# Decay matrices of a state-space scan: running sums spread by DMA and masked on GpSimd, in place of products on TensorE

## What is computed

```python
def _decay_matrix(a_cs):
    q = a_cs.shape[-1]
    mask = jnp.tril(jnp.ones((q, q), dtype=bool))
    diff = a_cs[..., :, None] - a_cs[..., None, :]
    return jnp.exp(jnp.where(mask, diff, -jnp.inf))
...
    decay_in = _decay_matrix(jnp.moveaxis(a_cs, 2, -1))
    cb = jnp.einsum('bclgn,bcsgn->bcgls', cc, bc)
    y_diag = jnp.einsum('bcgls,bcghls,bcsghp->bclghp', cb, decay_in, xdt)
    y_off = jnp.einsum('bclgn,bcghpn,bclgh->bclghp', cc, h_prev, jnp.exp(a_cs))
    return (y_diag + y_off).reshape(bsz, l, N_HEADS, HEAD_DIM)
```

## Time and profile before

| | us |
|---|---|
| median of 3 runs | 2501.23 |
| the runs | 2499.74, 2505.65, 2501.23 |
| the profiled execution: span of its instructions | 2505.4 |
| the profiled execution: its own time, the only one of the three that can hold the span | 2505.65 |
| PE busy, weight loads beside it | 2452.1, 1669.5 |
| DVE, ACT, POOL busy | 1099.7, 904.6, 167.6 |

### The profile page before, as it was taken

The page is one execution under the profiler, slowest core; times in us unless marked ns, Lnnn a source line. Parts: engine busy times, 40 slices in busy tenths (PEclk is TensorE's granted clock), DMA queues, the critical chain, the costliest instruction groups (busy, mean ns, idle before and its releaser), DMA issues.

```text
span 2505.4 us, 31969 instructions
## 1 busy us (share of the span) xinstructions
PE 2452.1 (98%) x13068; PEld 1669.5 (67%) x13068; DVE 1099.7 (44%) x1700; ACT 904.6 (36%) x1446; POOL 167.6 (7%) x162
## 2 busy tenths in 40 slices
PE   8999999999999999999999999999999999999998
PEld 7888778888888688898977888444444444444343
DVE  6446575455455755567866645221111111111111
ACT  5436454444444554466654643211101111101111
POOL 0000200000002000051600000000000000000000
PEclk9999999999999999999999999999999999999999
DMA  7546765555556665443422347999999999999997
GB/s 271 185 168 214 273 217 187 184 194 189 183 202 234 246 231 179 145 152 118 169 101 85 127 150 267 392 431 430 431 431 430 432 431 431 430 430 431 431 431 327
DMA packets 72805, 688.34 MB, mean 275 GB/s; under 512 B 8338, under 2 KB 8482, under 8 KB 12288
## 3 DMA queue, kind: packets, MB, share of 16 engines
q1 hardware_dynamic: 69696, 675.98, 69.1%
q0 software_dynamic: 3008, 10.95, 1.3%
HBM read 683.76 MB, written 1.05 MB: 273 GB/s over the span
## 4 chain that ended last, share of the span: by engine, by line
PE 82%; DMA 9%; DVE 4%; ACT 3%; issue 2%; POOL 0%; SPq 0%; ACTq 0%; DVEq 0%
PE bank L446 39%; PE bank L3018 21%; DMA work<-in_stream 4%; DMA ring<-in_stream 4%; PE bank L2965 4%; PE bank L1921 4%; PE bank L3007 2%; PE bank L484 2%; ACT split_r L401 1%; DVE work L1979 1%; PE bank L2321 1%; PE bank L764 1%; DVE ring_r L412 1%; PE bank L1100 1%; PE bank L1302 1%
## 5 line engine op out<-in xcount | busy, mean ns | idle before, releaser
L412 DVE TENSOR_TENSOR ring_r<-ring,split_r 128x2048 fp32r<-128x2048 f32 (+1 forms) x211 | 474.7, 2274 | 345.2 <-ACT split_r L401 345.1
L446 PE MATMUL bank<-split_r,xT_r 128*128 128x512 f32 (+1 forms) x1760 | 546.2, 388 | 1.8 <-ACT work L1426 1.7
L401 ACT CAST split_r<-ring 128x2048 fp32r<-128x2048 f32 (+1 forms) x228 | 429.3, 1904 | 160.3 <-PE bank L446 125.0
L446 PEld LDWEIGHTS bank<-split_r,xT_r 128*128 128x128 f32 x1760 | 328.7, 188 | 70.1 <-issue 2.3
L446 PE MATMUL bank<-ring_r,xT_r 128*128 128x512 f32 (+1 forms) x880 | 339.5, 386 | 0.0
L446 PE MATMUL bank<-split_r,work_r 128*128 128x512 f32 x960 | 301.0, 391 | 0.5 <-DVE ring_r L412 0.4
L3018 PE MATMUL bank<-ring,work 128*64 128x512 f32 x1152 | 261.1, 602 | 4.3 <-DMA ring<-in_stream 2.7
L446 PEld LDWEIGHTS bank<-split_r,work_r 128*128 128x128 f32 x960 | 180.3, 188 | 38.0 <-DVE ring_r L412 0.9
L446 PE MATMUL bank<-ring_r,work_r 128*128 128x512 f32 x480 | 186.9, 389 | 0.0
L446 PEld LDWEIGHTS bank<-ring_r,xT_r 128*128 128x128 f32 x880 | 165.4, 188 | 31.9
L3018 PEld LDWEIGHTS bank<-ring,work 128*64 128x64 f32 x1152 | 79.6, 138 | 154.8 <-issue 147.2
(11 more groups left out here) (409 smaller groups left out, 3063.7 us busy)
## 6 DMA issues: line engine op xcount, KB each, us to landing
ring<-in_stream SPq DMA_DIRECT2D x256, 1024.0 KB, 5.0
ring<-in_stream SPq DMA_DIRECT2D x72, 2048.0 KB, 27.0
split<-in_stream SPq DMA_DIRECT2D x48, 2048.0 KB, 27.8
xT<-in_stream SPq DMA_DIRECT2D x24, 2048.0 KB, 27.4
work<-in_stream SPq DMA_DIRECT2D x24, 2048.0 KB, 28.2
x<-in_stream SPq DMA_DIRECT2D x24, 1024.0 KB, 25.7
work<-in_stream SPq DMA_DIRECT2D x24, 1024.0 KB, 28.3
row<-in_rows POOLq DMA_DIRECT2D x6, 512.0 KB, 4.3
```

The source lines that it names most:

```text
L401: act.copy(hi, self.part(half, self.ring)).then_inc(*up("half_hi", half.h))
L412: dve.tensor_tensor(self.part(half, self.ring_lo), self.part(half, self.ring), hi.bitcast(F32), ALU.subtract).then_inc(*up("half_lo", half.h))
L446: mm = self.nc.tensor.matmul(out, a[x][a_at], w[y][w_at], start=start and n == 0, stop=stop and n == 2)
```

## The change

The running sums are now spread to all partitions by DMA. PE makes them once for each chunk and direction, with 64 rows. ACT copies them to SBUF as they are, POOL writes them to a DRAM tensor `acs_rows`, and for each unit POOL issues a DMA (`pool_seg`) that reads 8 rows of 128 and writes them to all 128 partitions: 4 KB a partition, 512 KB in all. There are three such buffers. POOL then adds the mask, in two halves of 128x512 (`pool_masked`), ACT takes the exponentials in place (`act_decays`), DVE multiplies in place (`dve_decays`), and the diagonal products read the same buffer. Units 0 and 1 use the space of the fourth split buffer, unit 2 the convolution's.

The mask and sum products leave PE, and DVE's `acs_lo` and `acs_wide` go. In unit u PE makes B times C of unit u + 1 after the state product, and ACT and DVE make the decays of unit u + 1: ACT after its split, DVE ahead of `y_sum`. `off` and the diagonal products change between two banks each, so their waits go back two units instead of one. POOL's order in the scan is: masks of u, then the DMA for u + 2, which waits for the diagonal products of u - 1. A few waits and constants move with it (the second gates wait for `cbT` 15 and `y_sum` 14 instead of the exponentials; a zero-weight tile is now written with the identity).

```diff
...
+        self.acs_rows = nc.dram_tensor("acs_rows", (2, MT * NH2, P), F32, kind="Internal").ap()
...
-                self.n_hi, self.hi_user[N_HI - 1] = N_HI, (-1, ("seg", 15, 1))
+                self.n_hi, self.hi_user[N_HI - 1] = N_HI, (-1, ("diag", 15))
...
-        self.acs_T = wr(12288, 2, P)
-        self.acs_wide = [view(self.split[N_HI - 1], d * 1024, 8, P) for d in range(2)]
+        assert at + 3 * KD + 3 * P <= self.base
+        self.acs_T = w(12288, 2, P)
+        self.seg = [view(self.split_f, (N_HI - 1) * HALF + i * 1024, 8, P) for i in range(2)] + [w(11264, 8, P)]
...
-        for src, dst in ((self.ident, self.ident_r), (self.con["neg_f"], self.neg_r[0]), (self.con["neg_b"], self.neg_r[1]),
-                         (self.con["group_of"], self.group_r)):
-            i = act.copy(dst, src)
-        i.then_inc(*up("masks", 0))
+        for i in range(MT):
+            act.copy(self.w_of_none[:, i * P:(i + 1) * P], self.ident)
+        act.copy(self.ident_r, self.ident).then_inc(*up("masks", 0))
...
         for m in range(MT):
-            for part in range(2):
-                rows = slice(64 * m + 32 * part, 64 * m + 32 * part + 32)
-                for d, tri in ((0, self.con["tri_f"]), (1, self.con["tri_b"])):
-                    mm = pe.matmul(self.bank[5][rows, d * P:(d + 1) * P], dA[:, m, d, :], tri, start=True, stop=True)
+            rows = slice(NH2 * m, NH2 * (m + 1))
+            for d, tri in ((0, self.con["tri_f"]), (1, self.con["tri_b"])):
+                mm = pe.matmul(self.bank[5][rows, d * P:(d + 1) * P], dA[:, m, d, :], tri, start=True, stop=True)
         mm.then_inc(*up("acs_turned", 0))
...
     def act_acs_hi(self):
         act, at, up = self.nc.scalar, self.s.at, self.s.up
         act.wait_ge(*at("acs_turned", 0))
-        act.copy(self.acs_T, self.bank[5][:, 0:2 * P].rearrange("p (d n) -> p d n", d=2)).then_inc(*up("acs_hi", 0))
-
-    def dve_acs_lo(self):
...
-    def dve_acs_wide(self, d):
...
+        rows = slice(0, MT * NH2)
+        act.copy(self.acs_T[rows], self.bank[5][rows, 0:2 * P].rearrange("p (d n) -> p d n", d=2)).then_inc(*up("acs_hi", 0))
+
+    def pool_acs_out(self):
+
+        pool, at, up = self.nc.gpsimd, self.s.at, self.s.up
+        pool.wait_ge(*at("acs_hi", 0))
+        pool.dma_start(self.acs_rows.rearrange("d r n -> r d n"), self.acs_T[0:MT * NH2]).then_inc(*up("dma_acs", 0))
+
+    def pool_seg(self, u):
+
+        pool, at, up = self.nc.gpsimd, self.s.at, self.s.up
+        d, m, g = self.units[u]
+        if u == 0:
+            pool.wait_ge(*at("dma_acs", 0))
+            pool.wait_ge(*at(*self.wide_after))
+        elif u == 2:
+            pool.wait_ge(*at("conv_turned", 55))
+        elif u > 2:
+            pool.wait_ge(*at("diag", u - 3))
+        rows = self.acs_rows[d, NH2 * m + 8 * g:NH2 * m + 8 * g + 8, :].rearrange("h n -> (h n)")
+        pool.dma_start(flat(self.seg[u % 3]), rows.partition_broadcast(P)).then_inc(*up(f"dma_seg{u % 3}", u))
+
+    def pool_masked(self, u):
+
+        pool, at, up = self.nc.gpsimd, self.s.at, self.s.up
+        d, m, g = self.units[u]
+        pool.wait_ge(*at(f"dma_seg{u % 3}", u))
+        for half in range(2):
+            e = self.seg[u % 3][:, 4 * half:4 * half + 4]
+            pool.tensor_tensor(e, e, spread(self.con["neg_b" if d else "neg_f"], 1, 4), ALU.add).then_inc(*up("masked", u, half))
 
...
-            elif n == 36:
-                self.dve_acs_lo()
-            elif n in (43, 45):
-                self.dve_acs_wide((n - 43) // 2)
...
         for h in self.by_pool:
+            if h == self.first_piece - 28 + 20:
+                self.pool_acs_out()
+            elif h == self.first_piece - 28 + 23:
+                self.pool_seg(0)
+                self.pool_seg(1)
             self.pool_split(h)
...
         pool.wait_ge(*at("h0", 0, 3))
         pool.wait_ge(*at("h0", 1, 3))
         for g in range(NG2):
+            if g == 2:
+                self.pool_masked(0)
             pool.wait_ge(*at("turn_out", 43 + 4 * g))
...
+    def pe_cb(self, u):
+        pe, at, up = self.nc.tensor, self.s.at, self.s.up
+        d, m, g = self.units[u]
+        tok = slice(m * P, (m + 1) * P)
+        if u:
+            pe.wait_ge(*at("cbT", u - 1))
+        pe.matmul(self.bank[2][:, 0:P], self.BT[d][:, g, tok], self.CT[d][:, g, tok], start=True, stop=True).then_inc(*up("cb", u))
+
     def pe_unit(self, u):
         pe, at, up, bank = self.nc.tensor, self.s.at, self.s.up, self.bank
         d, m, g = self.units[u]
         tok = slice(m * P, (m + 1) * P)
...
+        off, y = bank[4 + u % 2], bank[(3, 6)[u % 2]]
+        if u == 0:
+            for w in (("turn_out", 54), ("turn_out", 55), ("dt", "dX", 1), ("masks", 0), ("h0", 0, 3), ("h0", 1, 3)):
                 pe.wait_ge(*at(*w))
-        pe.matmul(bank[4][:, 0:P], self.BT[d][:, g, tok], self.CT[d][:, g, tok], start=True, stop=True).then_inc(
-            *up("cb", u))
-        for half in range(2):
-            if u:
-                pe.wait_ge(*at("dec_exp", u - 1, half))
-            pe.matmul(bank[2 + half][:, :].rearrange("p (h l) -> p h l", h=4), self.ident_r, spread(self.neg_r[d], 1, 4),
-                      start=True, stop=False)
-            mg = m * NG2 + g
-            pe.matmul(bank[2 + half][:, :].rearrange("p (h l) -> p h l", h=4), self.group_r[:, mg:mg + 1].broadcast_to([P, P]),
-                      self.acs_wide[d][:, 4 * half:4 * half + 4], start=False, stop=True).then_inc(*up("seg", u, half))
-        if u:
-            pe.wait_ge(*at("yo", u - 1))
+            self.pe_cb(0)
+        if u >= 2:
+            pe.wait_ge(*at("yo", u - 2))
         if u % 4 >= 2:
             pe.wait_ge(*at("h1", u - 2))
-        pe.matmul(bank[5][:, :], self.CT[d][:, g, tok], self.h_st[d][:, g * 512:(g + 1) * 512], start=True,
+        pe.matmul(off[:, :], self.CT[d][:, g, tok], self.h_st[d][:, g * 512:(g + 1) * 512], start=True,
                   stop=True).then_inc(*up("off", u))
         if u % 4 < 2:
             pe.wait_ge(*at("xw", u))
             if u >= 4 or u % 4:
                 pe.wait_ge(*at("h1", u - 1 if u % 4 else u - 3))
             pe.matmul(bank[7][:, :], self.B[:, d, g * P:(g + 1) * P], self.xw, start=True, stop=True).then_inc(*up("state", u))
+        if u + 1 < 16:
+            self.pe_cb(u + 1)
         for p in self.pieces[u] if u else ():
             self.pe_piece(p)
-        if u:
-            pe.wait_ge(*at("y_sum", u - 1))
+        if u >= 2:
+            pe.wait_ge(*at("y_sum", u - 2))
         for half in range(2):
             pe.wait_ge(*at("decay", u, half))
             for hh in range(4):
                 h = 4 * half + hh
-                mm = pe.matmul(bank[6][:, h * HD2:(h + 1) * HD2], self.dec[half][:, hh, :],
+                mm = pe.matmul(y[:, h * HD2:(h + 1) * HD2], self.seg[u % 3][:, h, :],
                                self.X[:, m, g * 512 + h * HD2:g * 512 + (h + 1) * HD2], start=True, stop=True)
         mm.then_inc(*up("diag", u))
 
+    def act_decays(self, u):
+        act, at, up = self.nc.scalar, self.s.at, self.s.up
+        d, m, g = self.units[u]
+        nb = self.T[1]["nb"]
+        if u == 0:
+            act.wait_ge(*at("dt", "nb"))
+        for half in range(2):
+            if half:
+                act.wait_ge(*at("cb", u))
+                if u >= 2:
+                    act.wait_ge(*at("decay", u - 2, 1))
+                act.copy(self.cbT[u % 2], self.bank[2][:, 0:P]).then_inc(*up("cbT", u))
+            act.wait_ge(*at("masked", u, half))
+            for hh in range(4 * half, 4 * half + 4):
+                e = self.seg[u % 3][:, hh, :]
+                i = act.activation(e, e, ACT.Exp, bias=nb[:, m, d, 8 * g + hh:8 * g + hh + 1])
+            i.then_inc(*up("dec_exp", u, half))
+
...
     def act_unit(self, u):
         act, at, up, bank = self.nc.scalar, self.s.at, self.s.up, self.bank
...
+        if u == 0:
+            self.act_decays(0)
         if u + 1 < 16:
             self.act_split(-(-self.pieces[u + 1].stop // 2) + self.first_piece - self.act_half)
+            self.act_decays(u + 1)
         else:
             self.act_split(1)
...
+    def dve_decays(self, u):
+        dve, at, up = self.nc.vector, self.s.at, self.s.up
+        d, m, g = self.units[u]
+        for half in range(2):
+            e = self.seg[u % 3][:, 4 * half:4 * half + 4]
+            if half == 0:
+                dve.wait_ge(*at("cbT", u))
+            dve.wait_ge(*at("dec_exp", u, half))
+            dve.tensor_tensor(e, e, spread(self.cbT[u % 2], 1, 4), ALU.mult).then_inc(*up("decay", u, half))
+
     def dve_unit(self, u):
         dve, at, up, bank = self.nc.vector, self.s.at, self.s.up, self.bank
         d, m, g = self.units[u]
+        off, y = bank[4 + u % 2], bank[(3, 6)[u % 2]]
         T, cols = self.T[1], slice(g * 512, (g + 1) * 512)
+        if u == 0:
+            self.dve_decays(0)
         if u % 4 < 2:
             if u:
```

(38 more changed lines are left out.)

30 lines of the change are left out of this document (removed).

## The result

The changed kernel takes 2537.67 us, the median of four runs (2536.66 to 2538.54), against 2502.43 for the kernel before in four runs: a ratio of 1.0139, 95% interval 1.0128 to 1.0151. That is 35.2 us slower. The direction was forecast, the size was not: 11.8 us had been said, and the time lies above the range.

The account below looks back on a forecast made before the run. PE, busy 2452.1 of 2505.4 us, was taken as the bound. -4.9 without new waits, +13.2 for pairs and +1.0 for unit 1 made +9.3; clock +2.5 made +11.8 on 2501.23: 2513.0 us, range 2494 to 2523.

Parts of the forecast that it names:

- The sum without new waits: Scan and projections: gains and losses on PE's path without POOL's new wait, -4.9 us in all, giving 2496.3 us.
- Exclusion between POOL's additions and DVE: Scan: POOL and DVE operations with two SBUF inputs fully block each other; each mask addition taken as 1.27 us.
- DVE keeping its turn while its operations follow each other: Scan: POOL's additions get in only when DVE's run of operations ends; with exclusion, chance 0.36.
- The walk: Step-by-step timing from the end of unit 2's diagonal products; state product of unit 4 starts at 12.1 us.
- first come, first served: Rival: a waiting POOL addition gets between y and xw, 1.27 us each in units 1, 5, 9, 13; 2518 us, chance 0.20.
- +13.2 of the three pairs: Unit pairs 3-4, 7-8, 11-12 each lose 4.4 us, state product at 12.1 instead of 7.7.
- Units 5, 9, 13 lose nothing in this order: The new wait costs these units 0; unit 1 alone loses +1.0 us, to skip products, DMA issue, masks and DVE's turns.
- Unit 0: Start of the scan: diagonal products end at 1277.7 against 1275.5 us, as DVE makes both decay halves ahead of xw(0): +2.1.
- The clock: Scan: PE at 1.2 instead of 2.4 GHz after waits, 1.7 us lost per pair; bounds 0 and 5.1, taken +2.5.
- The test named in the prediction: Profile signs: masks 1.2 to 1.3 us, lengthened DVE operations, PE idle up to 5 us in units 4, 8, 12, unit 2 shorter by 0.9.
- first come with all the clock loss: Label given to the upper end, 2523 us, of the range 2494 to 2523.
- late DMAs: Rival: DMAs landing in 8.5 us add 2 or 3 us in a short unit; four on top give 2523 us, chance 0.04.

## Why the prediction was right or wrong

- **The sum without new waits, -4.9**, held as far as the runs show it: the stretch without additions is 2.9 us shorter than before, with 13.7 us of half clock in it. Unit 6 takes 8.4 us against 9.3. PE's own work of unit 3 takes 5.6 us, as said; its recorded products end at 1306.6.
- **Exclusion between POOL's additions and DVE** was right in kind and in the price of one addition (1.25 to 1.29 us). The two additions took 2.5 us, 3.3 beside the held decays of units 4, 8 and 12; splits kept their 2.28 us.
- **The DMAs** were no matter, as costed. The group of the additions in the split's space, then that of the DMA issues and their landing (ns, min/median/max):

```profile
L2045 POOL TENSOR_TENSOR split<-split,work x20: 1262/1294/3388, 1269.7 to 1420.4; 128x512 f32<-128x512 f32 x20
```

```profile
L2036 POOL DMA_DIRECT2D split<-acs_rows x9: 568/568/571, 1280.1 to 1412.3; - x9
...
DMA to landing us min/median/max: 3.8/4.1/5.6
```

POOL waited for one of them once, for 1.7 us, at the start.
- **The turn was wrong.** "DVE keeping its turn while its operations follow each other" is the step that failed. The walk let `y` pass from 0.8 to 1.46 and put the additions behind it. `y` waited for both of them. The rival "first come, first served" had the right engine first, but one addition of 1.27 us between `y` and xw, where both, 2.5 us, came ahead of `y`.
- **For units 3 and 4 it made no difference.** The walk reached the state product of unit 4 at 12.1 us after the diagonal products of unit 2, and the trace has 12.4. Without additions it is 7.8 (7.7 in the prediction). Decays were late in the walk and in the trace; the late `y` took the place of the late split. So the +13.2 of the three pairs came out by another inner order than I gave, and that it fits is luck in part.
- **"Units 5, 9, 13 lose nothing in this order"** followed from the turn and fell with it. The state product of unit 5 starts 4.6 us after unit 4's diagonal products; the prediction's rows have 2.1. That is +2.5 each for units 1, 5, 9 and 13, some +10 where +1.0 stood.
- **Unit 0** came out later than the +2.1 said: the decays stood beside unit 1's additions (3.56 us for two, alone 1.3) and the diagonal products ran at half clock (3.32 us, before 2.07). From the first product to their end it is 12.7 us against 6.1.
- **The clock** was sized at +2.5 with 5.1 as its bound. It cost about 14 us, as measured by the kernel that keeps PE busy, and some 18 if its last 14 us of half clock cost as much. I had taken three places of 4 us at half clock; there were seven, since the waits I had left out bring it too, and each lasted 6.8 us or more. The wait costs twice: its own length, and some 2 us of slow products behind it.

Put together from the prediction's own terms: -4.9, +13.2 for the pairs, +10 for the `y` ahead of units 1, 5, 9 and 13, some +2 for unit 0's decays, +14 for the clock make +34; 35.2 was measured. The test named in the prediction would have told: `y` was expected at 1.3 to 2 us and came at 3.1, and PE's idle time of up to 5 us was expected in units 4, 8, 12 and came in eight units. One bound was mislabelled besides: "first come with all the clock loss" is 2518 + 2.6 = 2521, and the 2523 is the sum with late DMAs. The measured time is above both.

## What to carry to other kernels

Before an operation is given to POOL, look at what starts on DVE at the same event, and at what stands behind it in DVE's order. Here one event released both, and 0.8 us after it they met; a product on the critical path stood two operations further. Moving the operation that PE waits for ahead of the one that can be held was worth 31.7 us, and taking the additions away from that place as well another 10. And a wait on PE is to be priced with the slow products behind it: 37 us of waits brought some 15 more.

## What the runs showed of the hardware that was not expected

- A DVE operation recorded as starting 0.06 us ahead of POOL's pair of additions (in one kernel `h_decayed`, 0.45 us ahead) ended behind both. The Trainium skill, SBUF — State Buffer, section "Who interferes with whom", says that whoever issues first gets the shared pair for the whole instruction and the other blocks fully. The blocking agrees: 3.11 us is 2.5 of additions and 0.6 of work. The order, by recorded starts, does not; whether the recorded start is the moment of issue, no run here shows.
- It isn't that POOL always goes first. In the kernel with the additions after `y(u-2)`, splits that were asked for 0.55 us (three units) or 0.96 us (seven) after the first addition's start got in between the two, and the pair took 4.56 and 4.85 us. A split that had begun 0.24 us ahead of the additions, in the kernel with xw ahead and additions after `yo`, was not held (2.28 us); there the first addition waited and took 3.17 us. What tells these cases apart stays open.
- Four fp32 products of 3.60 us in all, put in a wait of 4 to 6 us, left no half clock at the waits of units 4, 5, 8, 9 and 13 and 3.4 us of it at unit 12's, where each had 6.8. Work without use on a waiting engine gave back 11 us. Those of unit 4 (timeline):

```profile
1305.42 3.60 PE L2320 MATMUL bank<-work 128*128 128x512 f32 x8
```
